# Expert rows gathered 64 tokens by two picks, two diagonals side by side on the array

## The chip, the cores and the metric

The kernel runs on one core of a Trainium2 chip. The metric is device time in microseconds of one execution, as the median of several runs. All numbers of hardware behaviour below are of this kernel's profiled execution or of its runs.

## What is computed

Two transformer blocks follow each other on 512 tokens of width 1024, in float32. The first ends with a layer of experts (PEER): every token picks 16 experts in each of 8 heads, 128 picks of 16384 experts, and adds up what they give:

```python
def chunk(args):
    hc, ec, gc = args
    u_sel = jnp.take(u, ec, axis=0)
    act = jax.nn.gelu(jnp.einsum('chkd,cd->chk', u_sel, hc), approximate=False) * gc
    v_sel = jnp.take(v, ec, axis=0)
    return jnp.einsum('chk,chkd->cd', act, v_sel)
```

The second block puts 16 meta tokens ahead and has a SwiGLU layer (width 2816), a mixer of retention and sparse attention, and another SwiGLU layer. It treats the sequence in two halves; the first half (256 tokens and the meta tokens) needs only the first half of the tokens.

## The kernel before

**Weights.** All dense weights come as slabs of 128 x 1024 float32 (512 KB), one after another on SyncE's queue. Each slab is split in two float32r parts: ScalarE rounds it (L1452) and VectorE, in places GpSimd, makes the remainder (L2279, L3244). TensorE multiplies in three passes (`Slab.add`, L715): 24 matmuls of 256 or 272 columns are one slab's product.

**Picks.** `peer_uv` holds for each expert its row of u and of v, 8 KB together. The 512 tokens are four tiles of 128, and a pick is one of the 128 choices of a tile: 512 picks in all, numbered n, which go through six slots (`uv_rows`, `SLOTS = 6`). For each pick

- GpSimd issues one indirect DMA (L3259) that brings 128 rows, 1 MB, one for each token; before that it waits until the slot's last user has told `uv_used`;
- VectorE multiplies the u halves with the tokens' rows `hrow` and sums (`dot`, L2571, the instruction is L2578);
- ScalarE makes gelu, the coefficient and a diagonal matrix of the 128 coefficients (`coefficient`, L1737: L1742, L1746, L1753);
- TensorE multiplies the diagonal with the v halves in two matmuls of 512 columns and adds up in two PSUM banks over the 128 picks of a tile (`weigh`, L1057: L1068). A float32 matmul is two passes with a weight load each, so a pick is four records of L1068.

**Tiles' ends.** After the last pick of a tile ScalarE (`take_sums`, L1756) or VectorE (`add_sums`, L2741) takes the two banks to `out_rows`, TensorE transposes them (`turn_rows`, L1075: L1082) and VectorE adds them to the residual `xT` (`add_rows`, L2581: L2586).

**Order.** Each engine has its own program, and the order is written by hand. Picks 0 to 255 (`PURE`, the first two tiles) are one **pure part**: one pick after the other, between them the rest of the first block for the second half of the tokens (`second_half`, at the picks in `STEPS`) and the choice of the experts of tiles 1 to 3 on VectorE (`choose_all`). Picks 256 to 511 are **woven** into the second block's first half, 261 slabs: when the program comes to slab t, VectorE makes the dots up to `woven_by(t)`, ScalarE the coefficients up to `woven_by(t - 1)`, and TensorE weighs the picks up to `woven_by(t - 3)` just ahead of the slab's product. `woven_by` gives one pick to a slab in the SwiGLU layers and six picks to five slabs in the mixer.

In the woven part every third pick of a tile (`by_dve`, 84 of 256) isn't weighed by TensorE: VectorE multiplies the v rows with the coefficient and adds them to `out_rows` (`add_row`, L2724: L2730, L2734). At the end of a tile in the woven part the next tile's picks are held back (`added_by`, `rows_by`): the sums are added at slab `TURN`, turned at `TURN + 2`, and the next tile's first picks are weighed at `TURN + 3`. `TURN` is slab 118 and slab 230.

## Time and profile before

| | |
|---|---|
| median of 3 runs | 3601.86 us (3600.21 to 3602.8) |
| profiled execution, from the first to the last instruction | 3601.5 us |
| pure part, first dot to the last pick's sums | about 750 to 1440 us |
| woven part | about 1470 to 2620 us |
| TensorE busy | 3316.3 us (92%) |
| VectorE busy | 2554.4 us (71%) |
| DMA, mean over the span | 255 GB/s |

The span is that of the slowest (only) core. The busy time of TensorE counts records, whose ends are modelled. A stretch's own limit has to be read from that stretch: which engine never stops, how much of the DMA engines' time is taken (share), and what the chain of waits passes through.

### The profile page before, as it was taken

To read this page: it belongs to the slowest core of one execution; us is meant where nothing else is said; L and a number is where in the kernel's file an instruction comes from. 1 tells how busy PE (TensorE), PEld (TensorE's weight loads), DVE (VectorE), ACT (ScalarE), POOL (GpSimd) and SP (SyncE) were. 2 spreads that over 40 slices of the span, in tenths; PEclk is the share of its full clock that TensorE was granted. 3 is DMA by queue.
4 is the path that set the end of the run, shared out by engine and by line. 5 is a ranking of instruction groups with operands and counts; after the bars stand their busy time and mean duration, and the time that the engine had idled before them with its cause. 6 is when DMAs were issued, how large, how long until landed. Compare 5 with 4: busy or idle time off the path is not lost.

```text
span 3601.5 us, 50492 instructions
## 1 busy us (share of the span) xinstructions
PE 3316.3 (92%) x18706; PEld 2633.5 (73%) x18706; DVE 2554.4 (71%) x4532; ACT 1537.0 (43%) x3089; POOL 770.5 (21%) x577
## 2 busy tenths in 40 slices
PE   7998889979898777799999999989999999999998
PEld 6886669855463222688777777767899988998898
DVE  6997143676777877687767777877867576768665
ACT  3222234245443333454444444545445443444443
POOL 1001236123435666122122122222200000000000
PEclk9999999999999999899899999999999999999999
DMA  3332224569999999699888899879956844453455
GB/s 123 94 95 75 75 83 141 182 272 397 407 415 421 417 411 418 261 377 389 324 321 312 305 372 385 317 296 341 374 176 188 267 141 131 133 184 106 140 184 156
DMA packets 184174, 918.82 MB, mean 255 GB/s; under 512 B 21536, under 2 KB 26912, under 8 KB 118128
## 3 DMA queue, kind: packets, MB, share of 16 engines
q0 software_dynamic: 73728, 536.90, 37.4%
q1 hardware_dynamic: 99248, 358.66, 29.9%
q10 hardware_dynamic: 10960, 20.12, 1.8%
q8 instruction: 145, 2.38, 0.3%
q14 instruction: 93, 0.76, 0.1%
HBM read 907.80 MB, written 7.80 MB: 254 GB/s over the span
## 4 chain that ended last, share of the span: by engine, by line
PE 72%; DVE 9%; DMA 7%; issue 5%; ACT 4%; POOL 2%; ACTq 0%; DVEq 0%; POOLq 0%
PE psum L715 54%; PE psum L1068 11%; DMA buffer_float<-in_peer_uv,buffer_uint 7%; DVE buffer_bfloat L2578 2%; POOL buffer_float L3259 2%; PE psum L1289 1%; ACT slabs_rounded L1452 1%; PE psum L723 1%; DVE buffer_float32r L2185 1%; PE psum L1274 1%; DVE norm_recip_root L2193 1%; DVE slabs_remainder L2279 1%; PE psum L1286 1%; PE psum L1372 1%; PE psum L1336 1%
## 5 line engine op out<-in xcount | busy, mean ns | idle before, releaser
L715 PE MATMUL psum<-buffer_float32r,slabs_rounded 128*128 128x256 f32 (+2 forms) x9568 | 2005.4, 309 | 70.3 <-POOL slabs_remainder L3244 30.1
L715 PEld LDWEIGHTS psum<-buffer_float32r,slabs_rounded 128*128 128x128 f32 x9568 | 1556.1, 192 | 217.3 <-issue 113.5
L715 PE MATMUL psum<-buffer_float32r,slabs_remainder 128*128 128x256 f32 (+2 forms) x4784 | 1439.8, 301 | 0.0
L2279 DVE TENSOR_TENSOR slabs_remainder<-raw_slabs,slabs_rounded 128x1024 fp32r<-128x1024 f32 x601 | 732.8, 1223 | 452.2 <-ACT slabs_rounded L1452 434.1
L1452 ACT ACTIVATE slabs_rounded<-raw_slabs 128x1024 fp32r<-128x1024 f32 x662 | 695.7, 1055 | 698.5 <-PE psum L715 620.7
L1068 PE MATMUL psum<-buffer_float,buffer_float 128*128 128x512 f32 x1712 | 825.2, 612 | 137.8 <-ACT buffer_float L1753 124.5
L715 PEld LDWEIGHTS psum<-buffer_float32r,slabs_remainder 128*128 128x128 f32 x4784 | 918.1, 192 | 29.8
L3259 POOL DMA_INDIRECT buffer_float<-in_peer_uv,buffer_uint x512 | 623.2, 1217 | 1330.8 <-PE psum L1068 753.6
L2578 DVE CUSTOM_DVE_ANT_0 buffer_bfloat<-buffer_float,buffer_float 128x1024 bf16<-128x1024 f32 x512 | 625.3, 1221 | 169.5 <-DMA buffer_float<-in_peer_uv,buffer_uint 160.8
L1068 PEld LDWEIGHTS psum<-buffer_float,buffer_float 128*128 128x128 f32 x1712 | 304.3, 193 | 519.6 <-issue 509.7
L1742 ACT ACTIVATE buffer_float<-buffer_float 128x1 f32<-128x1 f32 x512 | 100.3, 196 | 368.5 <-DVE buffer_float L2578 366.6
L3244 POOL TENSOR_TENSOR slabs_remainder<-raw_slabs,slabs_rounded 128x1024 fp32r<-128x1024 f32 x61 | 147.2, 2425 | 496.4 <-ACT slabs_rounded L1452 496.1
L1753 ACT ACTIVATE buffer_float<-fixed,buffer_float 128x128 f32<-128x128 f32 x428 | 172.1, 402 | 40.6 <-ACT buffer_float L1746 1.9
L715 PE MATMUL psum<-slabs_rounded,buffer_float32r 128*128 128x512 f32 (+1 forms) x608 | 184.2, 388 | 4.0 <-issue 4.0
L1436 ACT ACTIVATE buffer_float32r<-buffer_float 128x256 fp32r<-128x256 f32 (+3 forms) x224 | 104.0, 482 | 134.9 <-DVE buffer_float L2239 44.5
L2323 DVE SCALAR_TENSOR_TENSOR buffer_float<-buffer_float,vecs,buffer_float 128x512 f32<-128x512 f32 x232 | 158.9, 744 | 0.0
L1746 ACT ACTIVATE buffer_float<-buffer_float,buffer_float 128x1 f32<-128x1 f32 x512 | 150.9, 295 | 16.8
L2185 DVE TENSOR_TENSOR buffer_float32r<-buffer_float,buffer_float32r 128x256 fp32r<-128x256 f32 (+2 forms) x224 | 124.1, 568 | 19.8 <-ACT buffer_float32r L1436 18.1
L715 PEld LDWEIGHTS psum<-slabs_rounded,buffer_float32r 128*128 128x128 f32 x608 | 110.7, 190 | 36.4 <-issue 16.4
L715 PE MATMUL psum<-slabs_remainder,buffer_float32r 128*128 128x512 f32 (+1 forms) x304 | 113.3, 373 | 0.0
L2734 DVE SCALAR_TENSOR_TENSOR buffer_float<-buffer_float,buffer_float,buffer_float 128x1024 f32<-128x1024 f32 x82 | 105.0, 1281 | 0.0
L1837 ACT ACTIVATE buffer_float<-psum 128x256 f32<-128x256 f32 (+1 forms) x88 | 34.0, 386 | 103.4 <-PE psum L715 103.4
(213 smaller groups left out, 2039.0 us busy)
## 6 DMA issues: line engine op xcount, KB each, us to landing
raw_slabs<-in_slabs SPq DMA_DIRECT2D x682, 512.0 KB
buffer_float<-in_peer_uv,buffer_uint POOLq DMA_INDIRECT x512
buffer_float<-kept ACTq DMA_DIRECT2D x4, 874.5 KB, 6.0
xT<-in_xT ACTq DMA_DIRECT2D x4, 512.0 KB, 5.7
buffer_float<-in_consts ACTq DMA_DIRECT2D x8, 256.0 KB
kept<-buffer_float ACTq DMA_DIRECT2D x4, 512.0 KB
buffer_float<-kept ACTq DMA_DIRECT2D x2, 875.0 KB, 6.7
kept<-buffer_float ACTq DMA_DIRECT2D x4, 272.0 KB
```

Of the source, the lines that this page charges most:

```text
L715: m = pe.matmul(out, a, b, start=start and j == 0, stop=stop and j == 2)
L1068: m = pe.matmul(psum[:, b, :], diag[:, slot, :], uv_rows[slot][:, D + q * 512:D + (q + 1) * 512], start=p == 0, stop=p == PICKS - 1)
L1452: act.activation(slab_h[:, j, :], raw[:, r, :], ACT.Copy).then_inc(slab_rounded, 1)
L1746: act.activation(coefs[:, slot:slot + 1], acts[:, slot:slot + 1], ACT.Copy, scale=gates[:, tt, p:p + 1])\
L1753: act.activation(diag[:, slot, :], ident[:, :], ACT.Copy, scale=coefs[:, slot:slot + 1])\
L2185: dve.tensor_tensor(dst, src, high.bitcast(F32), ALU.subtract).then_inc(split, 1)
L2279: dve.tensor_tensor(slab_l[:, r, :], raw[:, r, :], slab_h[:, j, :].bitcast(F32), ALU.subtract)\
L2323: step(dve.scalar_tensor_tensor(out=acc, in0=cfp[:, h, t:t + S], scalar=w, in1=acc, op0=ALU.mult, op1=ALU.add))
L2578: dve.tensor_tensor_reduce(dump, uv_rows[slot][:, 0:D], hrow[tt], 1.0, 0.0, ALU.mult, ALU.add, dots[:, slot:slot + 1]).then_inc(dotted, 1)
L2734: ins = dve.scalar_tensor_tensor(out=out_rows, in0=v, scalar=c, in1=out_rows, op0=ALU.mult, op1=ALU.add)
L3244: pool.tensor_tensor(slab_l[:, r, :], raw[:, r, :], slab_h[:, j, :].bitcast(F32), ALU.subtract)\
L3259: pool.indirect_dma_start(uv_rows[slot], None, peer_uv_d, bass.IndirectOffsetOnAxis(eidx[:, tt, p:p + 1], 0))\
```

## The change

Gathered tiles hold 64 tokens instead of 128, and two picks of each: partitions 0 to 63 the even pick of the 64 tokens, 64 to 127 the odd one. A group of 64 tokens needs 64 gathers (`GROUP`), there are 8 groups (`GROUPS`), and still 512 gathers of 1 MB.

- The diagonal is 128 x 64: two identity matrices of 64 on top of each other (`stacked`), scaled by the coefficients. Its product with the v rows fills only 64 partitions of PSUM. `weigh_two` takes two gathered tiles at once: the first into partitions 0 to 63 of the bank, the second into 64 to 127, that is into different columns of the array. Both must have landed and have their diagonals, and both slots are told free in the second half of the pair.
- The sums' two halves are added up as they are turned: `turn_rows` is now a matmul of `out_rows` with `stacked`, into one bank.
- A tile's end comes after every 64 gathers: 8 times instead of 4. In the woven part `TURN` is slabs 63, 118, 171 and 230.
- `by_dve` takes every third of a group up to its 62nd: 80 of 256 instead of 84. TensorE weighs 176 in 88 pairs instead of 172.
- The tokens' rows must stand twice on the partitions. The first tile's are copied by ScalarE (`twin_rows`); those of the other three are written to DRAM (`rows_d`) and read back 64 at a time (`load_rows`, 6 times 2 DMAs of 256 KB), on ScalarE's queue.
- Indices and gates are written in four pieces instead of one.

```diff
+H64 = P // 2
+GROUP = PICKS // 2
+GROUPS = 2 * QT
...
-TURN = (turn_after(PICKS), turn_after(WOVEN))
-assert TURN[1] + 4 < BLOCK2, TURN
+BOUNDS = [GROUP * (j + 1) for j in range(WOVEN // GROUP)]
+TURN = [turn_after(n) for n in BOUNDS]
+assert TURN[-1] + 4 < BLOCK2, TURN
+
+
+def held(n, t):
+    for bound, turn in zip(BOUNDS, TURN):
+        if n > bound and t < turn + 3:
+            return bound
+    return n
...
-    return n >= PURE and n % PICKS % 3 == 2
+    return n >= PURE and n % GROUP % 3 == 2 and n % GROUP < GROUP - 2
...
+        rows_d = nc.dram_tensor("rows", (QT - 1, P, D), F32, kind="Internal").ap()
...
-        hrow = [early_rows[:, 0], early_rows[:, 1], late_rows[:, 0], late_rows[:, 1]]
-        diag = part(SLOTS, P)
+        hrow = [early_rows[:, 0], early_rows[:, 1], early_rows[:, 0], early_rows[:, 1],
+                late_rows[:, 0], late_rows[:, 1], late_rows[:, 0], late_rows[:, 1]]
+        diag = part(SLOTS, H64)
...
-            def weigh(n):
-
-                slot, turn, p = n % SLOTS, n // SLOTS, n % PICKS
-                if p == 0:
+            def weigh_two(*picks):
+                first, last = picks[0] % GROUP == 0, picks[1] % GROUP == GROUP - 1
+                if first:
                     sums_at[:] = [acc.take(), acc.take()]
-                pe.wait_ge(uv_landed[slot], 16 * turn + 16)
-                pe.wait_ge(diag_done, DIAGONALS[n + 1])
+                for n in picks:
+                    pe.wait_ge(uv_landed[n % SLOTS], 16 * (n // SLOTS) + 16)
+                pe.wait_ge(diag_done, DIAGONALS[picks[1] + 1])
                 for q in range(2):
                     b = sums_at[q][0]
-                    if p == 0:
+                    if first:
                         pe.wait_ge(bank_free[b], sums_at[q][1] + 1)
-                    m = pe.matmul(psum[:, b, :], diag[:, slot, :], uv_rows[slot][:, D + q * 512:D + (q + 1) * 512],
-                                  start=p == 0, stop=p == PICKS - 1)
-                    if p == PICKS - 1:
-                        m.then_inc(bank_full[b], 1)
-                if p < PICKS - 1:
-                    m.then_inc(uv_used[slot], 1)
-
-            def turn_rows(sums, turned):
-
-                for q in range(2):
-                    pe.wait_ge(bank_free[sums[q][0]], sums[q][1] + 2)
-                    pe.wait_ge(bank_free[turned[q][0]], turned[q][1] + 1)
-                    b = turned[q][0]
-                    for k in range(4):
-                        m = pe.transpose(psum[:, b, k * P:(k + 1) * P],
-                                         out_rows[:, (4 * q + k) * P:(4 * q + k + 1) * P], ident[:, :])
-                    m.then_inc(bank_full[b], 1)
-
-            first_sums = None
+                    for j, n in enumerate(picks):
+                        slot = n % SLOTS
+                        m = pe.matmul(psum[j * H64:(j + 1) * H64, b, :], diag[:, slot, :],
+                                      uv_rows[slot][:, D + q * 512:D + (q + 1) * 512], start=first, stop=last)
+                        if j and last:
+                            m.then_inc(bank_full[b], 1)
+                        elif q:
+                            m.then_inc(uv_used[slot], 1)
+
+            def turn_rows(sums, bn):
+
+                for b, n in sums:
+                    pe.wait_ge(bank_free[b], n + 2)
+                pe.wait_ge(bank_free[bn[0]], bn[1] + 1)
+                for k in range(KT):
+                    m = pe.matmul(psum[:, bn[0], k * H64:(k + 1) * H64], out_rows[:, k * P:(k + 1) * P], stacked,
+                                  start=True, stop=True)
+                m.then_inc(bank_full[bn[0]], 1)
...
-                weigh(n)
+                if n % 2:
+                    weigh_two(n - 1, n)
                 if n in STEPS:
                     next(steps)
-                if n == PICKS - 1:
-                    first_sums = list(sums_at)
-                if n == PICKS + 5:
-                    turn_rows(first_sums, [at.take(), at.take()])
+                if n % GROUP == GROUP - 1:
+                    last_sums = list(sums_at)
+                if n > GROUP and n % GROUP == TURN_AT:
+                    turn_rows(last_sums, at.take())
...
             def weigh_to(n):
 
                 while woven[0] < n:
                     if not by_dve(PURE + woven[0]):
-                        weigh(PURE + woven[0])
+                        waiting.append(PURE + woven[0])
                     woven[0] += 1
+                    if len(waiting) == 2:
+                        weigh_two(*waiting)
+                        waiting.clear()
...
+            def load_rows(g):
+
+                t, s = g // 2 - 1, g % 2
+                for c in range(2):
+                    act.dma_start(hrow[g][c * H64:(c + 1) * H64, :], rows_d[t, s * H64:(s + 1) * H64, :])\
+                        .then_inc(rows_here[s], 16)
...
+                if keep_as is not None:
+                    act.dma_start(rows_d[keep_as], rows).then_inc(rows_kept, 16)
...
+            def twin_rows():
+
+                for q in range(2):
+                    b = full(at.take())
+                    for g in range(2):
+                        for c in range(2):
+                            m = act.activation(hrow[g][c * H64:(c + 1) * H64, q * 512:(q + 1) * 512],
+                                               psum[g * H64:(g + 1) * H64, b, :], ACT.Copy)
+                            m.then_inc(bank_free[b] if g and c else rows_made, 1)
+                    act.wait_ge(rows_made, 3 * (q + 1))
...
-                act.activation(diag[:, slot, :], ident[:, :], ACT.Copy, scale=coefs[:, slot:slot + 1])\
+                act.activation(diag[:, slot, :], stacked, ACT.Copy, scale=coefs[:, slot:slot + 1])\
                     .then_inc(diag_done, 1)
+                g = n // GROUP + 2
+                if n % GROUP == GROUP - 1 and g < GROUPS and g not in (QT, QT + 1):
+                    if g == 2:
+                        act.wait_ge(rows_kept, 16)
+                    load_rows(g)
...
+                if n == LATE_ROWS:
+                    act.wait_ge(rows_kept, 16 * (QT - 1))
+                    load_rows(QT)
+                    load_rows(QT + 1)
...
-                step(dve.tensor_copy(eidx[:, tt, h0 * TOPK:h1 * TOPK], pk.fin_af[:, some].rearrange("p a b -> p (a b)")))
+                two = pk.fin_af[:, some].rearrange("p h (i c) -> p c (h i)", c=2)
+                for s in range(2):
+                    for c in range(2):
+                        step(dve.tensor_copy(eidx[c * H64:(c + 1) * H64, 2 * tt + s, h0 * TOPK // 2:h1 * TOPK // 2],
+                                             two[s * H64:(s + 1) * H64, c]))
```

**How the order of work moves, first place.** TensorE at the start of the woven part: the end of one slab's product (before L715, now L733, which is the same line), the picks that are weighed there (before L1068, now L1090), the next product. `buffer_float_111` to `_116` are the six slots, `buffer_float_103` the diagonals. Before:

```order
2263 L715 MATMUL psum<-buffer_float32r,slabs_rounded 128x272 x2
2264 L715 MATMUL psum<-buffer_float32r,slabs_remainder 128x272
2265 L1068 MATMUL psum<-buffer_float_115,buffer_float_103 128x512 x2
2266 L1068 MATMUL psum<-buffer_float_116,buffer_float_103 128x512 x2
2267 L1068 MATMUL psum<-buffer_float_112,buffer_float_103 128x512 x2
2268 L715 MATMUL psum<-buffer_float32r,slabs_rounded 128x272 x2
2269 L715 MATMUL psum<-buffer_float32r,slabs_remainder 128x272
...
2283 L715 MATMUL psum<-buffer_float32r,slabs_remainder 128x272
2284 L1068 MATMUL psum<-buffer_float_113,buffer_float_103 128x512 x2
2285 L715 MATMUL psum<-buffer_float32r,slabs_rounded 128x272 x2
```

Now:

```order
2522 L733 MATMUL psum<-buffer_float32r,slabs_remainder 128x272
2523 L1090 MATMUL psum<-buffer_float_115,buffer_float_103 64x512
2524 L1090 MATMUL psum<-buffer_float_116,buffer_float_103 64x512
2525 L1090 MATMUL psum<-buffer_float_115,buffer_float_103 64x512
2526 L1090 MATMUL psum<-buffer_float_116,buffer_float_103 64x512
2527 L733 MATMUL psum<-buffer_float32r,slabs_rounded 128x272 x2
2528 L733 MATMUL psum<-buffer_float32r,slabs_remainder 128x272
...
2542 L733 MATMUL psum<-buffer_float32r,slabs_remainder 128x272
2543 L1090 MATMUL psum<-buffer_float_112,buffer_float_103 64x512
2544 L1090 MATMUL psum<-buffer_float_113,buffer_float_103 64x512
2545 L1090 MATMUL psum<-buffer_float_112,buffer_float_103 64x512
2546 L1090 MATMUL psum<-buffer_float_113,buffer_float_103 64x512
2547 L733 MATMUL psum<-buffer_float32r,slabs_rounded 128x272 x2
```

Slot 112's pick was weighed one slab earlier, alone; now it waits for slot 113's pick and is weighed with it. Each row of the pair is one 64-partition product, and the two slots alternate.

**Second place.** ScalarE at pick 192 of the pure part (coefficients of one pick are the rows L1742, L1746, L1753, now L1791, L1796, L1803). Before:

```order
945 L1742 ACTIVATE buffer_float_109<-buffer_float_108 128x1
946 L1746 ACTIVATE buffer_float_110<-buffer_float_109,buffer_float_107 128x1
947 L1753 ACTIVATE buffer_float_103<-fixed,buffer_float_110 128x128
948 L1742 ACTIVATE buffer_float_109<-buffer_float_108 128x1
949 L1746 ACTIVATE buffer_float_110<-buffer_float_109,buffer_float_107 128x1
```

Now, with `buffer_float_97` the later rows of the tokens:

```order
953 L1791 ACTIVATE buffer_float_109<-buffer_float_108 128x1
954 L1796 ACTIVATE buffer_float_110<-buffer_float_109,buffer_float_107 128x1
955 L1803 ACTIVATE buffer_float_103<-fixed,buffer_float_110 128x64
956 L1681 DMA buffer_float_97<-rows 64x1024 x4
957 L1791 ACTIVATE buffer_float_109<-buffer_float_108 128x1
958 L1796 ACTIVATE buffer_float_110<-buffer_float_109,buffer_float_107 128x1
959 L1803 ACTIVATE buffer_float_103<-fixed,buffer_float_110 128x64
```

Four DMAs of 256 KB stand behind the pick's diagonal; two at a time stand behind picks 63, 127, 319 and 383, and three writes of 512 KB stand ahead of the pure part and in its first half.

## Rows read from the trace of the kernel before

**Rows 1.** Windows of all engines by stage: busy us (instructions), granted clock, DMA share, GB/s

```profile
750.00:1110.00 360.00, 331.72 (x1340) 196.34 (x1340) 263.09 (x571) 175.79 (x484) 145.15 (x125) 0.98 0.99 402
1110.00:1440.00 330.00, 255.32 (x533) 89.89 (x532) 264.37 (x692) 124.32 (x400) 210.42 (x132) 1.00 1.01 417
...
1480.00:1740.00 260.00, 259.73 (x1624) 215.53 (x1623) 198.43 (x282) 123.21 (x276) 64.53 (x65) 0.99 0.97 380
1740.00:2100.00 360.00, 341.73 (x1759) 262.08 (x1757) 257.63 (x398) 151.56 (x315) 72.05 (x70) 0.95 0.84 310
2100.00:2215.00 115.00, 114.97 (x657) 90.89 (x656) 91.34 (x126) 56.36 (x123) 34.83 (x31) 0.99 0.99 394
2215.00:2500.00 285.00, 259.47 (x1475) 203.59 (x1474) 223.94 (x384) 147.23 (x323) 65.07 (x61) 0.93 0.85 317
2500.00:2620.00 120.00, 119.41 (x794) 99.50 (x793) 96.84 (x141) 60.21 (x138) 24.61 (x25) 1.00 0.93 363
```

**Rows 2.** Timeline of two picks of the pure part: start us, us, engine, line, operation [idle before, releaser]

```profile
1299.98 1.23 DVE L2578 CUSTOM_DVE_ANT_0 buffer_bfloat<-buffer_float,buffer_float 128x1024 bf16<-128x1024 f32 x1 [0.84 <-DMA buffer_float<-in_peer_uv,buffer_uint]
...
1300.45 0.19 PEld L1068 LDWEIGHTS psum<-buffer_float,buffer_float 128*128 128x128 f32 x1 [0.24 <-issue]
...
1302.42 1.95 PE L1068 MATMUL psum<-buffer_float,buffer_float 128*128 128x512 f32 x4 [0.53 <-ACT buffer_float L1753]
...
1302.46 1.23 DVE L2578 CUSTOM_DVE_ANT_0 buffer_bfloat<-buffer_float,buffer_float 128x1024 bf16<-128x1024 f32 x1 [0.66 <-DMA buffer_float<-in_peer_uv,buffer_uint]
...
1302.71 1.79 POOL L3259 DMA_INDIRECT buffer_float<-in_peer_uv,buffer_uint  x1 [0.69 <-issue]
```

**Rows 3.** Chain of waits, end of the pure part, single pieces: start us, us, what

```profile
1350.88 1.74 POOL buffer_float L3259
...
1353.37 1.73 POOL buffer_float L3259
...
1414.28 9.40 DMA buffer_float<-in_peer_uv,buffer_uint
```

**Rows 4.** Chain of waits by line, the five stretches from 1480 us on, in their order

```profile
by line: PE psum L715 65.1%; PE psum L1068 29.1%; DMA raw_slabs<-in_slabs 3.8%; issue 0.5%; DVE buffer_bfloat L2578 0.5%; DVE buffer_float L2734 0.5%; ACT slabs_rounded L1452 0.4%; DVE buffer_float L2819 0.2%; DVE buffer_float L2815 0.1%; D
...
by line: PE psum L715 53.2%; PE psum L1068 22.6%; issue 4.2%; DMA buffer_float<-in_peer_uv,buffer_uint 3.8%; PE psum L1289 3.8%; PE psum L1286 2.8%; PE psum L1274 2.7%; PE psum L1231 1.4%; DVE buffer_bfloat L2578 0.7%; DVE buffer_float L273
...
by line: PE psum L715 69.5%; PE psum L1068 30.8%; issue 0.0%
...
by line: PE psum L715 31.0%; PE psum L1068 16.4%; issue 13.5%; DVE buffer_bfloat L2578 6.5%; ACT slabs_rounded L1452 4.6%; DVE buffer_float L2734 3.3%; ACT buffer_float L2015 2.0%; ACT L1742 1.8%; DVE buffer_float L3084 1.6%; DVE buffer_flo
...
by line: PE psum L715 47.7%; PE psum L1068 29.4%; issue 5.3%; DVE buffer_bfloat L2578 5.1%; DVE buffer_float L2734 5.0%; ACT slabs_rounded L1452 4.5%; DVE buffer_float L2819 1.8%; DVE buffer_float L2815 1.4%; DVE slabs_remainder L2279 0.1%;
```

**Rows 5.** Chain of waits, first SwiGLU layer: one pick

```profile
1515.93 1.72 PE psum L1068 x4
```

**Rows 6.** Timeline of TensorE at the first 64-row products (index scores)

```profile
1797.37 1.14 PE L1220 MATMUL psum<-buffer_float,buffer_float 64*128 64x256 f32 x8
1798.44 2.84 PE L1068 MATMUL psum<-buffer_float,buffer_float 128*128 128x512 f32 x6
```

**Rows 7.** Chain of waits at a product of eight 256-column passes on the whole array

```profile
1951.34 1.73 PE psum L1231 x8
```

**Rows 8.** The tile's end in the woven part: windows, as rows 1

```profile
2060.00:2070.00 10.00, 10.00 (x65) 8.15 (x63) 7.17 (x13) 4.60 (x11) 0.54 (x1) 1.00 0.61 214
...
2090.00:2100.00 10.00, 5.96 (x29) 4.02 (x27) 9.33 (x11) 4.92 (x10) 1.87 (x2) 0.79 1.00 394
```

**Rows 9.** Chain of waits behind that tile's end: the next gather

```profile
2073.58 5.57 DMA buffer_float<-in_peer_uv,buffer_uint
```

**Rows 10.** Window in which the granted clock fell, as rows 1

```profile
1440.00:1450.00 10.00, 3.58 (x18) 2.67 (x16) 4.68 (x11) 4.95 (x12) 0.93 (x1) 0.69 0.88 368
```

**Rows 11.** Timeline of VectorE ahead of the pure part: two small instructions that don't wait for each other

```profile
694.30 0.17 DVE L2505 TENSOR_SCALAR buffer_uint<-buffer_uint 128x16 uint32<-128x16 uint32 x1
694.38 0.17 DVE L2506 TENSOR_SCALAR buffer_uint<-buffer_uint 128x16 uint32<-128x16 uint32 x1
```

More of the change, by code:

```diff
@@ L234 @@
     DIAGONALS.append(DIAGONALS[-1] + (not by_dve(_n)))
[L235 removed]
+assert all(DIAGONALS[g * GROUP] % 2 == 0 for g in range(GROUPS + 1))
 def score_pieces(h):
@@ L1096, in _ @@
             assert next(steps, None) is None and slabs.value() == BLOCK1
-            turn_rows(list(sums_at), [at.take(), at.take()])
-            place, woven = [0], [0]
+            turn_rows(last_sums, at.take())
+            place, woven, waiting = [0], [0], []
             def weigh_to(n):
```

164 lines of the change are left out of this document (88 added, 76 removed).

## The prediction, made before the changed kernel was run

> **What bounds the kernel now.** I read the windows by stage first, since TensorE's 92% is a mean over stages with different limits. In both stretches of the pure part the DMA share is 0.99 to 1.01 at 402 to 417 GB/s, while TensorE is busy 255 of 330 us in the second [rows 1]: the gathers bound it. The timeline shows the same in one step: the dots start 2.48 us apart, that is 1.05 MB (128 rows of 8 KB) at 423 GB/s [rows 2]. The chain of waits there runs through the gathers (9.40 us) and through GpSimd's issues, 2.49 us apart with nothing waited for [rows 3]: issuing has no room either.
>
> The woven part is another case. From 1480 to 1740 and from 2100 to 2215 us TensorE never stops (259.73 of 260, 114.97 of 115), and the chain by line is L715 with L1068 [rows 1, 4]. But the DMA engines aren't idle: 380 and 394 GB/s at shares of 0.97 and 0.99. In the two mixer stretches (1740 to 2100, 2215 to 2500) there is more room, 310 and 317 GB/s, and part of the second's chain is VectorE, ScalarE and issue. So what the change takes from TensorE counts in the woven part alone, and where DMA is near its rate only up to that rate.
>
> **The pair on TensorE.** A pick is four passes in 1.72 us, 0.43 each [rows 5]; two picks are 3.44. How two 64-column products share the array no row shows. Bounds: all eight passes one after another, 3.44 us, and all side by side, 4 x 0.43 = 1.72. The nearest rows are the index scores, which use 64 rows of the array instead of 128: eight passes of 256 columns begin at 1797.37 and the next instruction at 1798.44, 1.07 us [rows 6], where eight such passes on the whole array take 1.73 [rows 7]. Half of 1.73 is 0.87; the other 0.20 is lost going in and coming out. I take the same for columns: 1.72 + 0.20 = 1.92, so a pair saves 1.52 of 3.44 us, 44% of L1068.
>
> The Trainium skill (TensorE: Matmul & The Clock Gate, packing small matmuls, measured speedup) gives 2.38 times for three column tiles. Taken in proportion, two give 1.59 times, a pair 2.17 us, and over 88 pairs the estimate would lose some 20 us of TensorE time against mine.
>
> **What of it counts.** L1068's share of the chain times the stretch, times 0.44 [rows 4]: 1480 to 1740: 0.291 x 260 = 76, gives 33 us; 1740 to 2100: 81, gives 36; 2100 to 2215: 35, gives 16; 2215 to 2500: 47, gives 21; 2500 to 2620: 35, gives 16. The bytes stay, so DMA caps each: at the 417 GB/s of the pure part the first stretch can shrink by 260 x (1 - 380/417) = 23, the third by 6, the fifth by 16; the mixer stretches have room. No mix of slabs and gathers holds 417 through and slots now come free later, so of the capped ones I take two thirds: 15, 4 and 10. In the mixer I take 30 of 36 (DMA would rise from 0.84 to 0.93) and 15 of 21 (the chain has other members close behind). Sum: **74 us less**. The ends are 0 and 122 (all five uncapped).
>
> **What it adds.**
> - *Groups' ends.* Two more in the woven part, at slabs 63 and 171. One costs, by the end at slab 118: TensorE idle 10 - 5.96 = 4.0 us between 2090 and 2100, after a stretch with a DMA share of 0.61 [rows 8]. Where DMA binds (slab 63) I take the lost 0.39 x 10 = 4 once more: 4 + 8 = **12 us** (4 to 20). VectorE's sums and TensorE's turning with two passes go with them; behind slab 63 and 171 the next picks are held, so a pick late there is what the next slab waits for. VectorE's four picks fewer are hidden.
> - *Tokens' rows through DRAM.* In the pure part two writes and four reads of 0.52 MB: 3.1 MB at 417 GB/s = **7.5 us** [rows 1], since DMA has nothing to spare there; the first write is ahead of it and the last two reads are in the mixer, at nothing (cover gone: 1.3 us each).
> - *The loop of six slots in the pure part.* A slot's round is 6 x 2.48 = 14.9 us. In it the gather takes 9.40 from issue to landing [rows 3], but a gather that finds the DMA engines less taken 5.57 [rows 9], so 3.8 us are slack. Now the first pick of a pair waits 2.48 for the second, and of the two slots told free together the second is issued 2.49 after the first [rows 3]. That leaves 1.3 us for every jitter of VectorE's and ScalarE's work. I take 2% of the 690 us, **14 us**; ends 0 and 60 (below).
> - *Ahead of the first pick* VectorE chooses head by head and now writes four pieces of indices instead of one, 8 x 3 more, and 3 of gates: small instructions that don't wait for each other start 0.08 us apart [rows 11], 27 x 0.08 = **2 us**. ScalarE's extra copies of the first rows lie beside this.
>
> Together 74 - 12 - 7.5 - 14 - 2 = 38 us less: 3601.5 - 38 = 3563.5 us by the profiled execution's span; the median of the runs is 0.4 above it. I say **3564 us**.
>
> **Rivals.**
> - *The slots' loop takes over in the pure part (slower).* A pair needs 1.92 us of TensorE in every 4.96, 39%. The granted clock is 1.00 there now with TensorE at 77%, but it fell to 0.69 in a stretch in which TensorE was busy 3.58 of 10 us [rows 1, 10], that is 1.2 instead of 2.4 GHz for most of it. At 1.2 GHz a pair takes 1.72 us more, and the 1.3 us of slack are gone: it decides as soon as the delay passes 3.8 us, and 2.48 + 1.72 = 4.2 does. If only half the slack is really there, each round of 14.9 is 4.2 - 1.9 = 2.3 longer, 0.38 a pick: 50 us over the second 132 picks, and half as much a pick, 23, over the first 124, which are slower anyhow (2.9 us a pick) but have matmuls of `second_half` between. 73 in place of 14: 3564 + 59 = **3623**. Against it: TensorE's pauses were longer there, and the DMA queue adapts.
> - *DMA binds the whole woven part but the mixer.* Then 15, 4 and 10 fall away: 3564 + 29 = **3593**. For it: shares of 0.97 and 0.99 now [rows 1].
> - *Weight loads of a pair can't be hidden.* They'd add 0.19 us [rows 2] to each of the four steps: 1.92 + 0.76 = 2.68, half the saving: 3564 + 37 = **3601**. Against it: the same rows show a 0.19 us load inside a running product of its own array, where a pick's four passes still take 1.72. The Trainium skill (same page, packing small matmuls, the mechanism) says that weight loads overlap matmuls only of another row group, and two column tiles share all rows; by that rule this is the case.
> - *The two don't run side by side at all.* A pair 3.44 + 0.20: in the woven part 88 x 0.20 = 18 slower instead of 74 faster, and the release comes 1.7 us later as at the low clock: 3564 + 92 + 59 = **3715**.
>
> **Chances.** Forecast 0.57 (its own range 3525 to 3594), slots' loop 0.20, DMA 0.10, weight loads 0.07, no sharing 0.06. About 0.2%, 7 us, is what a measurement of this kernel can tell. Faster: 0.57 and parts of the DMA case (0.05) and of the others (0.03), 0.65. Same: 0.03 of DMA, 0.05 of weight loads, 0.05 of the loop, 0.13. Slower 0.22. The range: no sharing (0.06) and the upper third of the loop (0.07) stay outside above, 0.05 below: **3515 to 3635**.
>
> **What would show it.** Right: L1068's successor in pairs some 1.9 us apart from the next instruction, its starts nearly together; the pure part 10 to 30 us longer at a DMA share near 1.00; the stretch from pick 256 to the last pick some 60 us shorter with higher GB/s; after it nothing changed. Wrong: a DMA share under 0.95 in the pure part with dots over 2.6 us apart (the slots' loop, with a low granted clock if that is its cause); pairs of 2.7 or 3.6 us; or TensorE waiting for gathers at slabs in which it never stopped.

## The result and the profile after

| | before | after |
|---|---|---|
| median | 3601.03 us (3598.45 to 3602.8) | 3666.72 us (3663.81 to 3677.51) |
| ratio | | 1.0192, 95% interval 1.0174 to 1.021 |
| span of the profiled execution | 3601.5 us | 3666.8 us |
| dot of pick 0 to dot of pick 255 (pure part) | 686.6 us | 757.0 us |
| dot of pick 256 to dot of pick 511 (woven part) | 1140.2 us | 1131.9 us |

The forecast was 3564 us, faster; the change is 66 us slower, outside the range. The dot of a pick is the `dot` instruction of VectorE (L2578, now L2646); its start marks where the kernel stands, and most of what follows is read with it. The windows by stage, as [rows 1], of the changed kernel (its stages begin later):

```profile
755.00:1120.00 365.00, 266.52 (x1344) 150.38 (x1344) 258.86 (x562) 167.30 (x473) 145.72 (x122) 0.87 0.98 388
1120.00:1510.00 390.00, 203.85 (x560) 53.27 (x560) 272.11 (x713) 119.56 (x406) 156.12 (x131) 0.70 0.95 362
1545.00:1800.00 255.00, 237.25 (x1677) 200.39 (x1676) 207.04 (x297) 128.17 (x295) 77.03 (x64) 0.99 0.97 390
1800.00:2165.00 365.00, 317.54 (x1808) 243.87 (x1808) 261.37 (x403) 155.21 (x326) 89.81 (x73) 0.91 0.83 310
2165.00:2280.00 115.00, 101.63 (x640) 80.43 (x639) 88.92 (x124) 51.10 (x117) 39.06 (x31) 0.99 0.98 395
2280.00:2565.00 285.00, 236.21 (x1462) 185.27 (x1461) 215.95 (x374) 142.16 (x316) 64.75 (x58) 0.89 0.81 307
2565.00:2685.00 120.00, 111.17 (x815) 93.36 (x813) 101.45 (x149) 61.30 (x142) 29.17 (x26) 0.99 0.96 384
```

The second line holds most of the pure part's loss: 390 us where before took 330, the granted clock down from 1.00 to 0.70 and 362 GB/s in place of 417. In the woven part TensorE is relieved in every stage (237 of 255 us busy where it never stopped), but the bytes a second rise only in the SwiGLU layers (380 to 390, 363 to 384 GB/s) and in the mixer not at all.

The pair itself came out close to the forecast. TensorE in the first SwiGLU layer, timeline:

```profile
1701.66 1.94 PE L1090 MATMUL psum<-buffer_float,buffer_float 128*64 128x512 f32 x8
1703.53 0.39 PE L733 MATMUL psum<-buffer_float32r,slabs_rounded 128*128 128x272 f32 x1
```

Eight passes take 1.87 us up to the next instruction (1.92 was the estimate; 3.44 for two picks by [rows 5]). But the products behind a pair are slower too. Chain of waits of the changed kernel, a pair and the three slabs' products behind it:

```profile
1701.73 1.87 PE psum L1090 x8
1703.60 9.21 PE psum L733 x72
```

The same of the kernel before, one slab's product and the next pick:

```profile
1512.92 3.01 PE psum L715 x24
1515.93 1.72 PE psum L1068 x4
```

Three slabs of 24 products would be 9.0 us and took 9.21. So a pair costs TensorE 1.87 + 0.2 = 2.07 us in all, and saves 1.37 of 3.44 where 1.52 was forecast.

One round of the slots' loop in the second half of the pure part, chain of waits (start us, us, what):

```profile
1188.47 9.25 DMA buffer_float<-in_peer_uv,buffer_uint
...
1197.74 1.23 DVE buffer_bfloat L2646
...
1200.13 3.66 PE psum L1090 x7
...
1204.58 0.94 POOL buffer_float L3326
1205.52 0.30 issue
1205.83 9.86 DMA buffer_float<-in_peer_uv,buffer_uint
```

From gather to gather 17.36 us for six picks, 2.89 a pick; in [rows 2] it was 2.48. The chain no longer runs along GpSimd's issues [rows 3] but through TensorE and back to a slot. The pair in it takes 3.66 us, nearly twice 1.87, at a granted clock of 0.70 for the stretch: it ran at 1.2 GHz, the lower of the two levels. The waits of the same stretch (1120 to 1510 us: engine, line, releaser: us, times, longest) say who waits:

```profile
POOL buffer_float L3326 <- PE psum L1090: 194.8, 51, 8.0
PE psum L1090 <- ACT buffer_float L1803: 188.6, 63, 7.2
```

Before, in the 320 us from 1120 to 1440, GpSimd waited 58.4 us for TensorE and TensorE 71.1 for diagonals. In the woven part TensorE's own waits moved in the same way (before from 1471, after from 1545 us; one line of each):

```profile
PE psum L1068 <- ACT buffer_float L1753: 7.9, 4, 4.0
```

```profile
PE psum L1090 <- ACT buffer_float L1803: 38.6, 16, 12.3
```

### The profile page after: what moved, and what is told of

Same layout as the page of the kernel before. It is cut to its first block, busy times and chain, and to the rows that moved or that the text cites. A ratio compares the mean times of both kernels' runs of the same rounds, so it can differ in the third digit from the quotient of the medians.

```text
span 3666.8 us, 50680 instructions
## 1 busy us (share of the span) xinstructions
PE 3102.5 (85%) x18818; PEld 2477.8 (68%) x18818; DVE 2562.0 (70%) x4577; ACT 1522.6 (42%) x3103; POOL 760.1 (21%) x577
## 4 chain that ended last, share of the span: by engine, by line
PE 58%; DMA 18%; DVE 12%; issue 6%; ACT 4%; POOL 2%; DVEq 0%; ACTq 0%; POOLq 0%
PE psum L733 45%; DMA buffer_float<-in_peer_uv,buffer_uint 15%; PE psum L1090 7%; DVE buffer_bfloat L2646 3%; DMA raw_slabs<-in_slabs 3%; POOL buffer_float L3326 1%; ACT slabs_rounded L1477 1%; PE psum L1314 1%; DVE buffer_float32r L2243 1%; DVE buffer_float L2802 1%; DVE slabs_remainder L2337 1%; PE psum L1299 1%; DVE norm_recip_root L2251 1%; DVE buffer_float L2297 1%; PE psum L1311 1%
## 5 line engine op out<-in xcount | busy, mean ns | idle before, releaser
L733 PE MATMUL psum<-buffer_float32r,slabs_rounded 128*128 128x256 f32 (+2 forms) x9568 | 1958.2, 304 | 85.8 <-POOL slabs_remainder L3311 30.1
L733 PEld LDWEIGHTS psum<-buffer_float32r,slabs_rounded 128*128 128x128 f32 x9568 | 1548.1, 193 | 246.8 <-issue 125.7
L733 PE MATMUL psum<-buffer_float32r,slabs_remainder 128*128 128x256 f32 (+2 forms) x4784 | 1440.4, 301 | 0.0
L733 PEld LDWEIGHTS psum<-buffer_float32r,slabs_remainder 128*128 128x128 f32 x4784 | 921.0, 193 | 29.4
L3326 POOL DMA_INDIRECT buffer_float<-in_peer_uv,buffer_uint x512 | 612.6, 1196 | 1414.8 <-PE psum L1090 847.5
L1090 PE MATMUL psum<-buffer_float,buffer_float 128*64 128x512 f32 x1728 | 537.0, 751 | 368.4 <-ACT buffer_float L1803 345.8
L2646 DVE CUSTOM_DVE_ANT_0 buffer_bfloat<-buffer_float,buffer_float 128x1024 bf16<-128x1024 f32 x512 | 625.9, 1222 | 291.4 <-DMA buffer_float<-in_peer_uv,buffer_uint 280.1
L1090 PEld LDWEIGHTS psum<-buffer_float,buffer_float 128*64 128x64 f32 x1728 | 134.8, 161 | 660.0 <-issue 638.1
L1791 ACT ACTIVATE buffer_float<-buffer_float 128x1 f32<-128x1 f32 x512 | 101.0, 197 | 520.8 <-DVE buffer_float L2646 519.9
L733 PE MATMUL psum<-slabs_rounded,buffer_float32r 128*128 128x512 f32 (+1 forms) x608 | 181.0, 384 | 19.0 <-issue 19.0
L1803 ACT ACTIVATE buffer_float<-fixed,buffer_float 128x64 f32<-128x64 f32 x432 | 150.4, 348 | 40.2 <-ACT buffer_float L1796 0.7
L1796 ACT ACTIVATE buffer_float<-buffer_float,buffer_float 128x1 f32<-128x1 f32 x512 | 150.9, 295 | 16.8
L733 PEld LDWEIGHTS psum<-slabs_rounded,buffer_float32r 128*128 128x128 f32 x608 | 111.4, 193 | 53.9 <-issue 33.0
L733 PE MATMUL psum<-slabs_remainder,buffer_float32r 128*128 128x512 f32 (+1 forms) x304 | 114.5, 376 | 0.0
L2802 DVE SCALAR_TENSOR_TENSOR buffer_float<-buffer_float,buffer_float,buffer_float 128x1024 f32<-128x1024 f32 x76 | 97.4, 1281 | 0.0
L741 PE MATMUL psum<-buffer_float,raw_slabs 128*128 128x256 f32 x320 | 73.4, 385 | 0.7 <-DVE buffer_float L2297 0.7
```

What stands on the lines that cost most here:

```text
L733: m = pe.matmul(out, a, b, start=start and j == 0, stop=stop and j == 2)
L1090: m = pe.matmul(psum[j * H64:(j + 1) * H64, b, :], diag[:, slot, :], uv_rows[slot][:, D + q * 512:D + (q + 1) * 512], start=first, stop=last)
L1796: act.activation(coefs[:, slot:slot + 1], acts[:, slot:slot + 1], ACT.Copy, scale=gate)\
L1803: act.activation(diag[:, slot, :], stacked, ACT.Copy, scale=coefs[:, slot:slot + 1])\
L2646: dve.tensor_tensor_reduce(dump, uv_rows[slot][:, 0:D], hrow[g], 1.0, 0.0, ALU.mult, ALU.add, dots[:, slot:slot + 1]).then_inc(dotted, 1)
L2802: ins = dve.scalar_tensor_tensor(out=out_rows, in0=v, scalar=c, in1=out_rows, op0=ALU.mult, op1=ALU.add)
```

## The experiments

A median is that of the timed runs; the parts are from one profiled execution each (dot 0 to 128, 128 to 255, 256 to 511). Nine traces have the changed woven program unaltered, or but for the order of one step; their woven parts lie between 1127.9 and 1140.2 us, so a trace alone tells nothing of less than 12 us there.

| kernel | median | 0 to 128 | 128 to 255 | 256 to 511 |
|---|---|---|---|---|
| before | 3601 | 365.9 | 320.6 | 1140.2 |
| changed | 3666.7 | 383.5 | 373.4 | 1131.9 |
| e1 single picks in pure part | 3607.3 | 365.6 | 334.1 | 1127.9 |
| e2 single picks everywhere | 3670.0 | 366.3 | 334.3 | 1183.5 |
| e3 before, half woven products | 3549.7 | 367.2 | 319.7 | 1090.3 |
| e4 before, half pure products | 3594.8 | 357.7 | 320.6 | 1139.4 |
| e5 / e14 / e15 / e13: 2, 3, 4, 6 fillers | 3662.5 / 3656.2 / 3659.7 / 3715.4 | 388.3 / 389.4 / 380.6 / 386.2 | 365.6 / 355.6 / 356.4 / 411.7 | 1128.0 / 1140.2 / 1138.3 / 1128.4 |
| e6 e1, sums folded first | 3607.9 | 367.7 | 332.3 | 1130.0 |
| e7 e1, no rows through DRAM | 3589.1 | 359.7 | 324.5 | 1122.9 |
| e8 e1, two woven ends | 3605.1 | 368.6 | 331.6 | 1114.0 |
| e9 e1, held for the partner | 3674.9 | 384.6 | 367.8 | 1129.2 |
| e10 wide pure part | 3593.8 | 366.9 | 326.0 | 1129.9 |
| e11 e3, held for the partner | 3553.5 | 365.1 | 321.7 | 1098.3 |
| e12 e10, two woven ends | 3587.8 | 366.5 | 322.1 | 1120.5 |

**Where the pairs cost and where they pay.** e1 weighs the pure part one 64-token pick at a time:

```diff
-                if n % 2:
-                    weigh_two(n - 1, n)
+                weigh_one(n)
```

> The changed kernel, but in the pure part each gathered tile is weighed alone as soon as it has landed and its slot is told free at once; the halves of the columns are used in turn. The woven part keeps its pairs. Theory 'pair wait' (the second pick of a pair holds the first one's slot, and the slots' loop then sets the pure part's pace): the pure part loses most of its 73 us, back to some 700 us (rows through DRAM remain, about 8 us): about 3605 us in all. Theory 'tokens' rows and group ends' (the extra transfers and the four ends instead of two cost the time): no change, about 3665. Theory 'columns' (a 64-column product is slower for other reasons): no change either, and passes over 0.43 us apart.

Measured: ratio 1.0023 (1.0012 to 1.0033). The pairs of the pure part alone cost 59 us. e2 takes them out of the woven part too (`weigh_one` in `weigh_to`).

> As e1_single_pure, and in the woven part too each tile is weighed alone at its own place; nothing shares the array. TensorE's time for picks is that of the kernel before (four passes, 1.72 us), the layout of 64 tokens, the eight groups and the rows through DRAM stay. If pairs are worth something in the woven part, this is slower than e1_single_pure by up to 60 us; if the pairs' late release eats what TensorE gains, it is equal or faster. Against the kernel before it shows what layout and group ends cost: expected 8 us in the pure part and 10 to 20 in the woven part, about 3625 us.

Measured: ratio 1.0191 (1.0174 to 1.0208), 63 us above e1: that is what pairs are worth against lone 64-column picks. It is also 45 us above what was expected of e2, and its woven part is 43 us longer than before. The expectation took 1.72 us for a pick, but a lone 64-column pick takes 1.86 up to the next instruction, and the slab behind it 3.19 instead of 3.01 (chain of waits):

```profile
1660.26 1.86 PE psum L1108 x4
1662.12 3.19 PE psum L733 x24
```

So it costs 2.05 us in all, and the 176 woven picks cost TensorE 176 x 2.05 - 172 x 1.72 = 65 us more than before. The narrow form is dear by itself, and most of what pairs win only pays that back.

**What relief of TensorE is worth.** e3 and e4 take the second of a pick's two products out of the kernel before (that half of the experts' output is left out), in the woven and in the pure part:

```diff
+                    if q and n >= PURE and 0 < p < PICKS - 1:
+                        break
```

> The kernel before; of the woven picks' two 512-column products the second is left out (but at a tile's first and last pick), so half of the v sums of the last two tiles are missing. A pick then takes TensorE 0.86 us, as in a pair, without pair wait and without more group ends. Theory 'TensorE bounds the woven part': 50 to 75 us faster, about 3535 us. Theory 'something else is close behind' (DMA in the SwiGLU layers, the heads' chains over VectorE and ScalarE in the mixer): 15 to 35 us faster, about 3575 us.

> The kernel before; in the pure part the second 512-column product of each pick is left out (but at a tile's first and last pick), so half of the v sums of the first two tiles are missing. TensorE is then as little busy there as with pairs, but each slot is told free at once. Theory 'clock': the granted clock falls as in the changed kernel (0.7), and the pure part is longer for it, 3620 us or more. Theory 'pair wait': the clock may fall but costs nothing, since a half pick at the low clock takes what a whole one takes now: 3601 us within 5.

e3: ratio 0.9852 (0.9836 to 0.9868), 50 us less. It takes 172 x 0.86 = 148 us off TensorE, the change 172 x 1.72 - 88 x 2.07 = 114, so with less relief than e3 the change should get less than 50. Two of e3's windows, as [rows 1]:

```profile
1480.00:1720.00 240.00, 224.77 (x1533) 198.79 (x1532) 196.76 (x280) 122.41 (x272) 80.33 (x65) 0.99 0.99 405
1720.00:2075.00 355.00, 318.93 (x1735) 259.02 (x1735) 267.11 (x409) 160.41 (x331) 82.24 (x75) 0.90 0.86 327
```

In the first stretch DMA takes over as forecast, in the mixer neither is full and the clock is below 1. e4: ratio 0.9985 (0.9975 to 0.9996). Its mean clock fell to 0.927 (before 0.971), to 0.66 in the second half of the pure part, and that half is as long as before. So a low clock there doesn't slow the pure part by itself, as long as a pick's TensorE time stays what it was: half a pick at the low clock takes what a whole one took at the full clock. A whole lone pick at the low clock was not run. The first half became 8 us shorter (357.7 for 365.9), so relief of TensorE was worth something there, against the prediction.

**The hold.** e9 is e1 with the wait of a pair: both products of the first pick are issued, then both of the second, when the second's diagonal is there (cut against e1).

```diff
-                weigh_one(n)
+                if n % 2:
+                    weigh_one(n - 1)
+                    weigh_one(n)
...
-                pe.wait_ge(diag_done, DIAGONALS[n + 1])
+                pe.wait_ge(diag_done, DIAGONALS[(n | 1) + 1])
```

> The kernel of the single-pick pure part (3607), whose lone products in the pure part are issued two and two: the first waits until the second pick's diagonal is made too. TensorE does the same work as there and its clock stays high, only the wait of a pair is added. If that wait on the loop of six slots is what the changed kernel pays, the pure part takes 45 to 60 us more than with lone products free to go (dot of pick 0 to dot of pick 255: 700 us there, 757 in the changed kernel) and the kernel 3650 to 3665. If the low clock or the sharing of the array is the cause, it stays within 10 us of 3607.

Measured: ratio 1.0213 (1.0197 to 1.0228), the pure part 52.7 us longer than e1's and within 5 of the changed kernel's. The wait brings nearly the whole loss with it. But e9 parts the hold neither from the clock, which did not stay high (0.76, third number from the right), nor from the sharing: in every pair of its pure part the two picks' passes ran side by side (see the last section), so it is nearly the changed kernel in another order of issue:

```profile
1200.00:1300.00 100.00, 51.91 (x140) 18.81 (x142) 79.82 (x179) 32.45 (x108) 37.60 (x33) 0.76 0.95 371
```

**The clock.** Four kernels put products with an all-zero stationary behind each pair of the second half:

```diff
+                    if n > PICKS and n % GROUP != GROUP - 1:
+                        for q in range(2):
+                            pe.matmul(psum[0:H64, sums_at[q][0], 0:FIXED], nothing[:, :], fixed[:, :],
+                                      start=False, stop=False)
```

> The changed kernel, and behind each pair of the second half of the pure part two products with an all-zero 64-column stationary (464 moving columns each, they add 0), so that TensorE is busier and its granted clock should stay high there; the pair still waits for its second pick. In the changed kernel picks 128 to 255 take 373 us (before 321, with single picks 334) at a granted clock of 0.68 to 0.74. If the low clock is what stretches the slots' loop (my rival's mechanism: 1.72 us more a pair), the clock goes to 0.95 or more and the 373 fall to 335 to 345, the whole kernel to 3625 to 3640. If the wait for the second pick does it alone, the clock goes up and the stretch stays 365 to 375, the kernel at 3660 to 3670.

Ratio 1.0167 (1.0146 to 1.0187). Only half a test: clock 0.88 from 1200 to 1300 us, and a third of the pairs still slow (23 of 64 took over 2.5 us). So six:

> The changed kernel with six filling products behind each pair of the second half of the pure part instead of two (an all-zero stationary, they add 0), so that TensorE is busy nearly all of the time between pairs. With two the clock rose to 0.87 only, a pair there still took 2.47 us on average (3.10 in the changed kernel, 1.94 at the full clock), and picks 128 to 255 took 365.6 us instead of 373.4. If clock and hold work together as in my rival (either alone is within the slack), the clock goes over 0.95, a pair takes about 1.95 and the stretch falls to 325 to 340: kernel 3620 to 3635. If the hold of 2.5 us is by itself more than the slack, the stretch stays at 350 to 362 and the kernel at 3642 to 3658. If the filling products get in the pairs' way: over 366.

Ratio 1.0321 (1.0299 to 1.0342); a miss of my sizing. Its chain is TensorE's pairs (L1092) and fillers (L1117) almost alone, 97% of it from 1200 to 1400 us:

```profile
1203.14 4.28 PE psum L1117 x11
...
1207.81 1.72 PE psum L1092 x7
1209.53 4.28 PE psum L1117 x11
```

Three and four leave room:

> The changed kernel with three filling products behind each pair of the second half of the pure part. Six took 4.67 us a pair and made TensorE itself the bound (picks 128 to 255 in 412 us, every cycle 6.39 us); three are 2.34 us, with the pair 4.1 to 4.3 of the 5 us that two gathers take. If clock and hold work together, the clock is over 0.95, a pair 1.95 us and the stretch 325 to 345 (373 in the changed kernel, 334 with lone products, 321 before): kernel 3615 to 3635. If the hold by itself is more than the slack, 350 to 362: 3642 to 3658.

> The same with four filling products, 3.12 us a pair, with the pair 4.84 to 5.06 us of TensorE in a cycle: its clock can't fall any more, but TensorE is near its own bound. If clock and hold work together: the stretch 328 to 345, kernel 3618 to 3636. If the hold by itself is more than the slack: 350 to 365, 3642 to 3660.

Ratios 1.0165 (1.0145 to 1.0184) and 1.0179 (1.016 to 1.0198); both stretches 356 us. The same window in e14, and a round of its loop at the full clock:

```profile
1200.00:1300.00 100.00, 77.37 (x252) 25.53 (x251) 82.27 (x187) 33.31 (x111) 45.17 (x36) 0.98 0.96 379
```

```profile
1223.88 8.81 DMA buffer_float<-in_peer_uv,buffer_uint
...
1232.71 1.23 DVE buffer_bfloat L2654
...
1235.10 1.92 PE psum L1092 x7
...
1237.81 1.89 POOL buffer_float L3334
1239.70 0.30 issue
1240.01 8.62 DMA buffer_float<-in_peer_uv,buffer_uint
```

The pair is back at 1.92 us and the round still takes 16.13, where six gathers need 14.9. With a pair at some 2.2 us on average (3.0 in the changed kernel) the stretch gives back 17 to 18 of the 39 us that pairs add to e1's 334; 22 stay. The fillers themselves are not what stays: in e14 61 of the 64 pairs of this half begin within 0.3 us of the second pick's diagonal (62 in the changed kernel), and what they begin later than the usual 0.14 us sums to 5.9 us, against 2.3. So both parts of my rival are real, but its threshold isn't: the hold is over the slack without the clock.

**The tokens' rows.** e7 is e1 without the writes and reads of `rows_d` and the waits for them (picks of later groups use earlier tokens' rows).

> The kernel of the single-pick pure part (3607), without the tokens' rows going through DRAM: no writes, no reads and no waits for them (the picks of the third group on then use the first groups' rows, so that part of the computation is other). Its pure part is 15 us longer than before; the forecast put 7.5 of it on this traffic. If all 3.1 MB wait in line: 3598 to 3600 with the pure part 7 to 8 shorter. If the waits for rows at a group's start add to it: the pure part 11 to 15 shorter, 3592 to 3596.

Ratio 0.9967 (0.9956 to 0.9978), 18 us below e1, 15 of them in the pure part, more than either case expected of the whole. Most lie where the reads are: e1's dots fall behind e7's by 6.6 us at the four reads of 1288 us (1 MB), by 2.6 and 3.2 at the two pairs of reads before. The windows of e1 there and of e7 at the same picks:

```profile
1288.00:1298.00 10.00, 6.68 (x16) 1.78 (x16) 6.85 (x34) 2.89 (x11) 4.59 (x5) 1.00 1.02 338
1298.00:1308.00 10.00, 4.90 (x7) 1.30 (x8) 6.12 (x25) 1.69 (x6) 2.02 (x2) 0.80 1.01 328
```

```profile
1276.00:1286.00 10.00, 7.15 (x17) 1.86 (x16) 9.61 (x45) 4.46 (x14) 6.66 (x4) 1.00 1.01 420
```

The DMA engines are just as busy (1.01) and move 333 instead of 420 GB/s for 20 us. 1 MB at 417 would be 2.5 us.

**The groups' ends.** e6 puts `add_sums` ahead of the slab's dots in VectorE's `point`; e8 lets the sums run over 128 gathers (`BOUNDS` in steps of `PICKS`; those picks' output is put together otherwise).

> The kernel of the single-pick pure part (3607), with VectorE's folding of a finished group's sums put ahead of the dot of the next pick, which waits for its gather. If that wait is what makes a group's end dear (the two new ends cost 10 and 12.6 us there, the old one 2.8 more), each of them gets 3 to 5 us cheaper: 3592 to 3602. If it is the 16 turning passes and the held picks, it stays within 3 of 3607.

> The kernel of the single-pick pure part (3607), with two group ends in the woven part as in the kernel before instead of four: the sums run over 128 gathers, no fold and no turning after the first and third group there (the output of those picks is put together otherwise). Forecast's term: two ends cost 12 us, so 3595. If they cost what the dot times say, some 24 us: 3583. If what is lost at an end is made up in the slabs behind it, over 3600.

e6: 1.002 (1.001 to 1.003), no gain. e8: 1.0011 (0.9996 to 1.0026), 2 us below e1; its ten runs fell into two heaps, three at 3590 to 3593 and seven at 3603 to 3609, with the profile in the lower one, so e12 asked again on the quieter base of e10:

> The version with the wide pure part (3594), with two group ends in the woven part instead of four, as in the run on two ends (whose times fell into two heaps, 3590 to 3593 and 3603 to 3609, so that its median says 2 us for the two ends and its trace 12): the sums run over 128 gathers, the output of those picks is put together otherwise. If the two further ends cost what the dot times say (8 to 9 us at each, part of it made up behind): 3576 to 3586. If they cost next to nothing in the end: 3590 to 3596.

Ratio 0.9962 (0.9947 to 0.9976): 6 us for two ends. At an end itself the dots lose 7 to 9 us by e1 against e8 and 5 to 6 by e10 against e12; behind the first end 6 of them were made up in the former, none in the latter.

**The hold in the woven part.**

> The kernel before with the second half of each woven product left out (3550, its woven part 50 us shorter), and with the woven picks weighed two and two: the first waits for the second's diagonal. It prices the wait of a pair in the woven part without the two further ends and the rows. If holding a pick for its partner is what keeps the change's woven part from the 50 us, most of it goes: 3575 to 3590. If not, it stays at 3550 to 3560 and the ends and rows carry the rest.

Ratio 0.9885 (0.9863 to 0.9907), 4 us above e3 by the medians and 8 by the dots: there a pick may wait for its partner at little cost.

**The wide pure part with the paired woven part.** e10 keeps the old pure part (128 tokens a gather, a 128-column diagonal in a ring of four, two ends), has the new woven part, and puts the reads of the first woven rows behind the last pure pick:

```diff
+                if n < PURE:
+                    if n >= WIDE:
+                        act.wait_ge(uv_used[(n - WIDE) % SLOTS], (n - WIDE) // SLOTS + 1)
+                    act.wait_ge(coef_done, n + 1)
+                    act.activation(wide[:, n % WIDE, :], ident[:, :], ACT.Copy, scale=coefs[:, slot:slot + 1])\
...
-                if n == LATE_ROWS:
-                    act.wait_ge(rows_kept, 16 * (QT - 1))
+                if n == PURE - 1:
+                    act.wait_ge(rows_kept, 32)
```

> A version made from what the runs so far say: the pure part as before the change (128 tokens to a gather, a 128-column diagonal, two tiles' ends, no rows through DRAM but the two writes for the last two tiles, 1 MB), the woven part as changed (64 tokens by two picks, pairs, four ends); the reads of the first woven rows go behind the last pure pick, where the DMA engines have room. Pure part within 5 us of before (the two writes), woven part 12 to 17 us shorter: 3586 to 3596. If the woven part's gain depended on what precedes it: 3600 or more.

Ratio 0.9981 (0.9971 to 0.9991) to before: 6 us, about what a measurement of this kernel can tell, with the interval below 1, and 73 us faster than the change as made. Its windows in the pure part, to be read beside those of the changed kernel above:

```profile
755.00:1120.00 365.00, 333.25 (x1350) 196.40 (x1349) 264.35 (x576) 177.13 (x486) 148.73 (x128) 1.00 1.00 404
1120.00:1440.00 320.00, 248.49 (x510) 88.81 (x509) 258.54 (x685) 117.78 (x380) 194.06 (x126) 0.98 1.00 409
```

Clock and DMA share are back at 0.98 and 1.00; of its pure part's 6.4 us over before, two writes of rows (1 MB, 2.5 us at the full rate) are part, the rest isn't assigned.

## Why the prediction was wrong

By the dots the miss of 103 us lies in both parts. The pure part took 70 us more than before where 21.5 were forecast, the woven part 8 less where 62 were (74 less the ends' 12). Two steps failed, the slots' loop and the woven part, and one term was too small, the rows. (The five terms sum to 38.5, not 38; that is half a microsecond.)

**The pair: nearly right.** 1.87 us up to the next instruction, but 2.07 with what the products behind it lose, against 1.92; my estimate from [rows 6] stopped at the next instruction. 2.07 lies between it and the 2.17 of the estimate in proportion. Over 88 pairs the 0.15 is 13 us of TensorE time. The rival of weight loads that can't be hidden fell with it; by the rule of the Trainium skill (TensorE: Matmul & The Clock Gate, packing small matmuls, the mechanism) that a weight load overlaps only products of another row group, it would have come true, and the measurement decides: two column halves share all rows and the steps take 0.43 us, the first 0.48. The in-and-out time of some 0.33 us is paid by a lone pick too (e2's 2.05 against 1.72), so a pair replaces 4.10, not 3.44, if the 64-column form is taken as given.

**The slots' loop: the first step that failed.** I wrote 14 us and its rival 73; pairs cost 59. The failed number is the slack of 3.8 us, taken as 9.40 less the 5.57 of a gather that found the DMA engines less taken [rows 3, 9]. The chain of a full loop shows none that short: in e14's, at the full clock, gathers of 8.2 to 9.1 us stand in the chain from 1200 to 1275 us, at a DMA share of 0.96. A round is then 8.8 (gather) + 1.23 (dot) + 1.2 (ScalarE) + 1.9 (pair) + 0.8 + 1.9 (issue of the pair's first slot) and 0.3: 16.1 us, over the 14.9 of six gathers. The first slot's issue stands ahead of the second's gather because both slots come free together. Without it the round is 14.2 us, so by this round the slack is about 0.7 us (an estimate) instead of 3.8. My "that leaves 1.3 us" was below zero. The rival had the mechanism (chance 0.20), but with the same slack as a threshold: 4.2 over 3.8. The runs show hold alone about 22 of the 39 us in the second half, the low clock on top of it 17. For the first half (18 us) they aren't parted.

**The tokens' rows: 7.5, measured 18** (15 in the pure part). Bytes over rate is no price for them: the rate itself falls while they are read. Why these 64-partition reads are dear, no run tells.

**Groups' ends: 12, measured 6 (e12) or 2 (e8).** Half or less, inside its range of 4 to 20 for e12; the dots at an end (5 to 9 us each) overstate it.

**Indices, gates and the first rows: 2.** The first dot came 2.5 us later; right.

**The woven part: the second step that failed.** 74 us of relief were forecast and 62 with the two ends; 8 came. e3 shows that even more relief gives 50. Read at the five stages' bounds of before, e3's dots gained 17 us (forecast 15), 16 (30), 2 (4), 9 (15) and 6 (10), those of the changed kernel 14, 0, -1, -11 and 6. So the stretches where DMA caps came out near the forecast, and the failed terms are the mixer's 30 and 15: 25 in e3, nothing left of them in the changed kernel. There I let 30 of 36 us through since DMA had room and TensorE filled the chain; but the chain of a full TensorE doesn't show who is next. What is next is seen in the accounts of TensorE, from windows of 10 us over the woven part; what a clock under 1 took is busy time times one less the clock:

| | before | e3 | changed |
|---|---|---|---|
| length | 1140 | 1090 | 1132 |
| idle | 49 | 119 | 136 |
| taken by a clock under 1 | 37 | 56 | 49 |
| work | 1054 | 915 | 947 |

Of 107 us less work 87 became idle time and 12 went to the lower clock. TensorE's largest single wait is for diagonals (38.6 us; 32.4 in e3), and a diagonal needs its pick's gather and dot. In the first mixer stretch VectorE's dots waited 8.9 us for gathers before, 12.3 in e3 and 36.4 in the changed kernel, at a DMA share of only 0.83. So the picks themselves are late next, and not because the DMA engines are full; that their slots come free later is my reading and no run shows it. The further 42 us from e3 to the changed kernel are in part: hold 4, ends 6, rows 3, and 107 instead of 139 us less work, in proportion 12. Some 17 are not accounted for; the 12 us that traces of the same woven program differ by are part of that.

## What to carry to other kernels

A ring of buffers has as its slack its period less all steps of one round, with the latency that a transfer has *while the ring is full* (here 14.9 less 14.2 us); a short transfer seen in a quiet moment is no bound for it. What makes a slot's user wait for a second slot then costs time, here even with TensorE idle for half of it (52 of 100 us busy), so pair only where the ring isn't the bound (59 us were lost in the pure part). And price the narrow form too: in the woven part pairs won 63 us against lone 64-column picks, but only 8 to 12 of its length by the dots against the 128-column picks of before, since a 64-column pick costs 2.05 us alone and a 128-column one 1.72. And when relief of the busiest engine is to be priced, first take its work out and run that: one run (e3) would have said 50 at most instead of 74.

## What was not expected of the hardware

- **Products in different column halves overlap without being interleaved.** In e9 the kernel issues all four passes of one pick, then all four of the next, the two in different halves of the columns. They ran as a pair does, here at the full clock:

```profile
834.97 1.94 PE L1108 MATMUL psum<-buffer_float,buffer_float 128*64 128x512 f32 x8
```

Eight passes in 1.94 us, starting two and two 13 ns apart; the last passes of both picks, known by the semaphores that they tell, start at 836.303 and 836.316. In all 128 pairs of e9's pure part the two picks' passes alternate; in most the second pick's start some 0.12 us behind the first's. The Trainium skill (same page, what overlaps and what doesn't) has products strictly in program order; this trace differs.

- **The reads of rows took the DMA engines' time at a worse rate** (328 to 343 GB/s at a share of 1.01 to 1.03, against 420).
- **A low clock outlasted the waits between pairs.** With two fillers behind each pair 23 of the 64 pairs of the second half still took over 2.5 us, with three 12, with none 43.
